# Where the decode values of the undilated cached keys are multiplied: TensorE bank or VectorE passes

## The reference, cut to what matters

```
B_PATTERNS = ((128, 1), (512, 4), (2048, 16))
idx = lc + jnp.arange(t)[:, None] - jnp.arange(n_keys)[None, :] * dil     # which rows a query reads
o = jnp.einsum('bhtj,btjhd->bhthd' ..., p, kvg[:, :, :, 1])               # probabilities times values
o = jnp.einsum('gbsh,gbshd->bshd', w, outs)                              # sum of the groups
```

## Time and profile before

| | |
|---|---|
| median of 3 runs | 1751.55 us |
| lowest, highest | 1749.12, 1754.42 us |
| the profiled execution's own time | 1753.26 us |
| its span, first to last instruction | 1751.2 us |
| TensorE matmul busy | 1695.2 us, 97% |
| VectorE busy | 987.7 us, 56% |
| ScalarE busy | 700.4 us, 40% |
| mean granted TensorE clock | 0.983 |

### The profile page before, as it was taken

The page is one execution under the profiler, slowest core; times in us unless marked ns, Lnnn a source line. Parts: engine busy times, 40 slices in busy tenths (PEclk is TensorE's granted clock), DMA queues, the critical chain, the costliest instruction groups (busy, mean ns, idle before and its releaser), DMA issues.

```text
span 1751.2 us, 32475 instructions
## 1 busy us (share of the span) xinstructions
PE 1695.2 (97%) x12511; PEld 1639.1 (94%) x12511; DVE 987.7 (56%) x1371; ACT 700.4 (40%) x1041; POOL 117.0 (7%) x217
## 2 busy tenths in 40 slices
PE   8999999877999999999999999999999999999997
PEld 7999999755999998999999999999999999999996
DVE  4457667664487776666775444444445445445545
ACT  4434434364443333343444334444333333333333
POOL 1012222332011000000000000000000000000000
PEclk9999999987999999999999999999999999999999
DMA  6579999765577776668678788777687887657661
GB/s 215 154 242 325 328 316 337 248 188 188 196 263 241 242 260 199 209 219 261 205 236 263 244 275 251 252 241 242 218 272 239 257 270 251 190 162 246 196 190 54
DMA packets 204397, 410.75 MB, mean 235 GB/s; under 512 B 11900, under 2 KB 105366, under 8 KB 200096
## 3 DMA queue, kind: packets, MB, share of 16 engines
q1 hardware_dynamic: 178384, 254.41, 45.3%
q10 hardware_dynamic: 7488, 91.33, 15.9%
q0 software_dynamic: 18448, 63.93, 11.0%
HBM read 403.47 MB, written 94.92 MB: 285 GB/s over the span
## 4 chain that ended last, share of the span: by engine, by line
PE 91%; ACT 3%; DVE 2%; DMA 2%; issue 1%; ACTq 0%; POOL 0%; SPq 0%; DVEq 0%; POOLq 0%
PE bank L1365 89%; PE bank L1368 3%; ACT SP L710 1%; ACT SP L699 1%; DMA xs_s<-in_x_sample_dram 0%; DMA raw<-in_w_in_dram 0%; DVE U L1279 0%; DMA KA<-in_cache_a_dram 0%; DVE U L1272 0%; DMA QST<-tok_scratch 0%; ACTq L598 0%; ACT FT L648 0%; DMA BIAS<-bias_scratch 0%; DMA tok_scratch<-TOKS 0%; DVE RS L1298 0%
## 5 line engine op out<-in xcount | busy, mean ns | idle before, releaser
L939 DVE TENSOR_TENSOR wlo<-raw,whi 128x1024 fp32r<-128x1024 f32 x473 | 576.6, 1224 | 631.4 <-ACT whi L623 630.9
L623 ACT ACTIVATE whi<-raw 128x1024 fp32r<-128x1024 f32 x473 | 499.7, 1061 | 826.4 <-PE bank L1365 669.7
L1365 PE MATMUL bank<-X1H,whi 128*128 128x288 f32 x1408 | 417.0, 296 | 1.8 <-DVE X1L L1286 1.6
L1365 PE MATMUL bank<-X1L,whi 128*128 128x288 f32 x1408 | 415.4, 295 | 0.0
L1365 PE MATMUL bank<-X1H,wlo 128*128 128x288 f32 x1408 | 414.0, 294 | 0.0
L1365 PE MATMUL bank<-XH,whi 128*128 128x288 f32 x1248 | 375.2, 301 | 0.7 <-issue 0.5
L1365 PE MATMUL bank<-XL,whi 128*128 128x288 f32 x1248 | 369.6, 296 | 0.0
L1365 PE MATMUL bank<-XH,wlo 128*128 128x288 f32 x1248 | 368.5, 295 | 0.0
L1365 PEld LDWEIGHTS bank<-X1H,whi 128*128 128x128 f32 x1408 | 263.8, 187 | 2.5 <-issue 2.0
L1365 PEld LDWEIGHTS bank<-X1H,wlo 128*128 128x128 f32 x1408 | 265.2, 188 | 0.0
L1365 PEld LDWEIGHTS bank<-X1L,whi 128*128 128x128 f32 x1408 | 264.3, 188 | 0.0
(11 more groups left out here) (240 smaller groups left out, 1591.6 us busy)
## 6 DMA issues: line engine op xcount, KB each, us to landing
raw<-in_w_ffn_in_dram SPq DMA_DIRECT2D x176, 512.0 KB, 4.7
raw<-in_w_in_dram SPq DMA_DIRECT2D x156, 512.0 KB, 5.0
out_dram<-in_cache_b_dram ACTq DMA_DIRECT2D x28, 2336.0 KB, 11.6
raw<-in_w_ffn_out_dram SPq DMA_DIRECT2D x88, 512.0 KB, 4.6
KST<-in_cache_b_dram POOLq DMA_DIRECT2D x32, 512.0 KB, 5.0
QST<-tok_scratch POOLq DMA_DIRECT2D x32, 512.0 KB, 6.4
VST<-in_cache_b_dram POOLq DMA_DIRECT2D x16, 1024.0 KB, 6.1
raw<-in_w_out_dram SPq DMA_DIRECT2D x32, 512.0 KB, 5.2
```

The costliest lines, as they stand in the source:

```text
L623: nc.scalar.activation(whi[s][:, :], raw[s][:, :], ACT.Copy).then_inc(hi_done, 1)
L939: nc.vector.tensor_tensor(wlo[s][:, :], raw[s][:, :], whi[s][:, :].bitcast(F32), ALU.subtract).then_inc(lo_done, 1)
L1365: return nc.tensor.matmul(out, lhsT, rhs, start=start, stop=stop, **kw)
```

## The change

VectorE's step with C1 and one of the two adds go; PV is made directly from VST[0]. Three passes are left, behind the splits k = 2, 4, 6 of gates 1 to 7, and behind k = 5, 6, 7 of gate 0. The first of them now carries the wait for `pv_used`. TensorE gets four matmuls per sequence: the weights are 128 x 128 blocks of C1 (two heads), the moving operand is 8 columns of PTB (the two heads' probabilities for 4 tokens), and they accumulate into bank 4. They stand between the matmuls with CA and the wait for `pv_ready`, and the last of them now signals `cv_used`.

```diff
-                        pool.wait_ge(*((vp_done, 4 * b - 1) if g == 1 else (pv_ready, b)))
+                        pool.wait_ge(*((vp_done, 2 * b - 1) if g == 1 else (pv_ready, b)))
...
-                if step in (0, 3):
-                    g = step // 3
-                    dve.wait_ge(v_in[g], 16 * b + 16)
-                    nc.vector.tensor_tensor(heads(VST[:, g]), heads(VST[:, g]), p(1 + g), ALU.mult).then_inc(vp_done, 1)
-                elif step == 2:
-                    dve.wait_ge(vp_done, 4 * b + 2)
-                    nc.vector.tensor_tensor(PV[:, :, :], PV[:, :, :], VST[:, 0], ALU.add).then_inc(vp_done, 1)
-                elif step == 1:
-                    dve.wait_ge(cv_in[par], 32 * loads)
+                if step == 0:
+                    dve.wait_ge(v_in[0], 16 * b + 16)
                     if not known_below(b, 1):
                         dve.wait_ge(pv_used, b)
-                    v = C1[:, par].rearrange("p (h d) -> p h d", h=BH).unsqueeze(1).broadcast_to([P, DS, BH, DH])
-                    nc.vector.tensor_tensor(heads(PV[:, :, :]), v, p(0), ALU.mult).then_inc(vp_done, 1)
+                    nc.vector.tensor_tensor(heads(PV[:, :, :]), heads(VST[:, 0]), p(1), ALU.mult).then_inc(vp_done, 1)
+                elif step == 1:
+                    dve.wait_ge(v_in[1], 16 * b + 16)
+                    nc.vector.tensor_tensor(heads(VST[:, 1]), heads(VST[:, 1]), p(2), ALU.mult).then_inc(vp_done, 1)
                 else:
-                    dve.wait_ge(vp_done, 4 * b + 4)
+                    dve.wait_ge(vp_done, 2 * b + 2)
                     nc.vector.tensor_tensor(PV[:, :, :], PV[:, :, :], VST[:, 1], ALU.add).then_inc(pv_ready, 1)
...
-                for step in ((), (), (), (), (), (0,), (1, 2), (3, 4))[k]:
-                    value_products(0, 1, 0, step)
+                if k >= 5:
+                    value_products(0, 1, 0, k - 5)
...
-                    if 2 <= k < 7:
-                        value_products(b, loads, par, k - 2)
+                    if k in (2, 4, 6):
+                        value_products(b, loads, par, k // 2 - 1)
...
+                for pr in range(4):
+                    ins = mm(bank[4][:, 64 * pr:64 * pr + 64].rearrange("p (h b t) -> p h b t", h=2, t=DS)[:, :, b, :],
+                             C1[:, b % 2, P * pr:P * pr + P],
+                             PTB[:, 0].rearrange("p c r -> p (c r)")[:, 32 * b + 8 * pr:32 * b + 8 * pr + 8]
+                             .rearrange("p (h t) -> p h t", t=DS), False, False, skip_group_check=True)
                 ins.then_inc(cv_used, 1)
                 pe.wait_ge(pv_ready, b + 1)
```

## The result

The changed kernel's median is 1757.99 us over 14 runs (1753.94 to 1762.01), the kernel before's in the same comparison 1750.92 us (1747.24 to 1754.42): ratio 1.0040, 95% interval 1.0029 to 1.0051, so 7.1 us slower (5.1 to 8.9). The forecast was 7.4 us slower.

The account below looks back on a forecast made before the run. The prediction took TensorE's unbroken stream as the bound: 0 for VectorE's removed passes, 7.4 us for the added matmuls, 0 for moved waits and loads, so 1751.55 + 7.4 = 1759.0 us; 8-in-10 range 1753.5 to 1763.5.

Parts of the forecast that it names:

- The bound: Gates stage: TensorE's unbroken stream sets the time; VectorE waits for ScalarE, ScalarE for TensorE, with VectorE 6.7 us spare per period.
- Removed: VectorE's 16 dropped passes, 36.5 us, lie beside TensorE's unbroken piece and return 0, at most 0.8 us.
- Added: TensorE's C1 matmuls, 64 records in 8 blocks of 0.93 us (VN's whole block), paid in full: 7.4 us.
- The prediction's sum with one change more, 8.2 us: TensorE's C1 blocks if each sequence paid one more tiling-mode switch, which drains the engine: 8.2 us in all.
- The moved wait: VectorE's first pass, behind split k = 2, stands 3.2 us until TensorE has read the old PV; cost 0.
- The slack of 6.0 us: Time left before TensorE needs chunk k + 3 = 6, whose split ends 3.3 us late through the wait for PV.
- The other moved signals and loads: Later `cv_used`, earlier VST[0] load, C1's load sharing CA's semaphore, and PV ready earlier: all cost 0.
- Rival 1: C1's weight loads hide under running TensorE matmuls: 2.8 us less 0.8, 1753.6 us, no measurable change; chance 0.14.
- Rival 2: Short C1 matmuls make the clock fall once in each of 8 blocks, 3.4 us each: 1786 us; chance 0.04.
- Rival 3: The earlier wait for PV reaches TensorE through late `wlo` or raw, up to 23 us: 1782 us; chance 0.04.
- Rival 4: VectorE is a hidden bound; its relief shortens TensorE's piece by more than 7.4 us, e.g. 1746.8 us; chance 0.04.
- the likeliest case: The whole kernel slows by the C1 matmuls' 7.4 us on TensorE, to 1759.0 us; chance 0.74.

Follow-up runs that it names:

- The addition alone: The kernel before with the four C1 matmuls per sequence added on TensorE and all five VectorE passes kept: ratio 1.0039, +6.8 us.
- the relief alone: The changed kernel without its C1 matmuls, so three VectorE passes and no new TensorE work: ratio 1.0001 to the kernel before.
- the doubled kernel: The changed kernel with the four C1 matmuls per sequence issued twice: ratio 1.0160 to the kernel before, +28 us.

## Why the prediction was right

- **The bound.** Right: the order of waiting (VectorE for ScalarE for TensorE) and the unbroken piece said that VectorE's time is free here. The addition alone measured 1.0039, the relief alone 1.0001, the whole 1.0040.
- **Removed, taken as 0.** Right. The bound of -0.8 us was not used either. VectorE's busy time fell by 33.1 us, not 36.5: a pass overlaps its neighbours by 0.08 to 0.09 us at either end, which the sum of durations counts twice (up to 16 x 0.17 = 2.7 us of the 3.4).
- **Added, 8 x 0.93 = 7.4 us.** The mechanism was right, the size 0.06 us per block low: 0.99 us, 7.8 us on the chain. VN's records, from which it was taken, have the same pace, but VN's block stands behind a chunk with weights as wide as its own, and C1's between two narrower shapes. KB's 0.116 was read from a whole count of 11 in 1.276 us, VN's is a block's mean; in the traces the records of both, and those with C1, start 0.109 to 0.112 us apart once a block runs. The estimate of 107 ns (the Trainium skill, TensorE: Matmul & The Clock Gate, LDWEIGHTS) is within 5% of that. What the Trainium skill says there, that the columns of the weights count, agrees with the run with 64-wide weights: 0.058 us from one record to the next in the same column half. The interval of the measured +7.1 us holds both 7.4 and 7.8, so that the forecast came within 0.3 us of the median is partly luck.
- **The change of tile shape.** It costs about 0.1 us, and shows in CA's block, 0.26 us with the next block of its own shape and 0.35 us with another. The prediction's sum with one change more, 8.2 us, is about as far above the trace's 7.8 as 7.4 is below it.
- **The moved wait.** Right in size (3.44 us for 3.2) and in effect (none). The slack of 6.0 us was tested from the other side: a first pass one split earlier still costs nothing, two splits earlier costs 0.6 us per gate. The other moved signals and loads, taken as 0, are in the relief's 1.0001 too.
- **Rival 1 (hidden loads)** is out in the form of the change and half true in another: with 64-wide weights the same work costs 3.7 us on the chain. **Rival 2 (clock)** did not happen in the change (1.00 in every stretch of 5 us from 470 to 685 us) and does when the block is doubled; its price per fall was 1.7 us there, not 3.4, since a fall lasted 3.4 us and not 6.8. **Rival 3** is out at the place of the change. **Rival 4** is out by the relief alone.
- **The range.** The text gives 1755.5 to 1763 us for the likeliest case; with its own bounds, 2.8 and 8.6, and the spread of the runs the lower end would be 1752 us. The 1758.0 measured lies well inside either.

## What to carry to other kernels

Before work is moved to TensorE from an engine at 56%, look at who waits for whom in that stage: here the bigger-looking saving was 33 us of free time, the cost 8 us of the only time that counts. The small float32 matmuls here, with 8 to 64 moving columns, are paid by the width of their weights, so 64-wide weights in separate column halves beat half as many 128-wide ones, even with twice the records. That holds while few columns move: with 32-wide weights and 128 moving columns 8 records took 0.99 us as well. In this kernel a gap of 2.5 us, and in half the gates a stretch of 16 thin records, cost twice, once itself and once in the half clock that went with it. Dense filler in a gap that had to be waited out was free here.

## What was not expected of the hardware

- The clock's fall in a stream that never idles: TensorE busy 5.00 of 5.00 us in the records, and still clock 0.68, from the end of CA and 16 records of 8 columns on. With 128 columns in the second 8 records the like stretch kept 1.00.
- 128-wide weights: about 0.112 us from record to record with 8, 32, 64 or 128 moving columns (in the changed kernel, in those with 32 and with 128 columns, and at VN). 64-wide weights in two column halves: 0.034 us per record (0.55/16), against 0.124 (0.99/8).
- How often the clock falls differs between executions of the same kernel: the doubled kernel's ranged from 1770.43 us at mean clock 0.982 to 1782.64 us at 0.975.
